# A two-layer hybrid decoder: the causal mask added on VectorE, one product for the av squares, sums and waits moved

## What is computed

```
h = rms_norm(x);  p = h @ W_in
A: u = gelu(a_u);  v = rms_norm(gelu(a_v));  y = u * (tril(w_s[g]) @ v + b_s)      # 8 groups, 4 chunks of 128 tokens
B: q, k, v from normalised latents, rotary on 32 of 96 columns, 8 heads
   softmax(q k^T * scale + causal mask) @ v                                         # 4 query blocks of 128
C: gated DeltaNet: conv(4) + silu, l2-normalised q and k, chunks of 64, 8 heads
x = x + (sum_i sigmoid(gate_i) * (y_i @ W_branch[i])) @ W_out
x = x + W2 relu(W1 rms_norm(x))^2
```

## Times and profile before

| | before |
|---|---|
| median of 3 runs | 1871.1 us (1866.58 to 1871.3) |
| the profiled execution | 1870.5 us, span 1868.7 us |
| PE busy | 1839.4 us, 98% of the span |
| DVE, ACT, POOL busy | 874.4, 467.7 and 1030.7 us |
| mean granted clock of PE | 0.994 |

### The profile page before, as it was taken

How to read it: one execution, slowest core, us unless ns; L and a number is a source line. 1 busy time by engine, 2 the same in 40 slices (tenths; PEclk the granted TensorE clock), 3 DMA queues, 4 the chain that set the end, 5 groups by cost and what they waited for, 6 DMA issues and landing times.

```text
span 1868.7 us, 26963 instructions
## 1 busy us (share of the span) xinstructions
PE 1839.4 (98%) x10428; PEld 1496.6 (80%) x10428; DVE 874.4 (47%) x1283; ACT 467.7 (25%) x872; POOL 1030.7 (55%) x580
## 2 busy tenths in 40 slices
PE   8999999999999999999999999999999999999998
PEld 7787788768888888888888777887788888888887
DVE  7787545554354322323266855465434542314141
ACT  6433314560114000000154242165501230000010
POOL 6444177225666666666654523662366666666662
PEclk9999999999999999999999999999999999999999
DMA  6212122122223232232332211321222323232332
GB/s 231 76 61 69 36 90 102 46 80 91 91 90 114 92 102 93 99 100 93 101 136 68 68 58 46 98 94 35 91 90 90 102 90 102 91 102 92 100 97 73
DMA packets 46762, 167.12 MB, mean 89 GB/s; under 512 B 5018, under 2 KB 8346, under 8 KB 46146
## 3 DMA queue, kind: packets, MB, share of 16 engines
q1 hardware_dynamic: 44066, 154.30, 24.9%
q10 hardware_dynamic: 2592, 11.29, 1.6%
HBM read 159.28 MB, written 6.29 MB: 89 GB/s over the span
## 4 chain that ended last, share of the span: by engine, by line
PE 88%; DVE 8%; ACT 2%; issue 1%; DMA 0%; SPq 0%; ACTq 0%; DVEq 0%
PE ps L445 25%; PE ps L447 25%; PE ps L446 25%; PE ps L899 2%; PE ps L922 1%; DVE lanes L1660 1%; PE ps L909 1%; DVE ps L1676 1%; DVE outer L1673 1%; PE ps L535 1%; PE ps L710 1%; PE ps L678 1%; DVE convd L1567 1%; DVE acc L1448 1%; PE ps L688 1%
## 5 line engine op out<-in xcount | busy, mean ns | idle before, releaser
L408 POOL TENSOR_SCALAR wHi<-wraw 128x1024 fp32r<-128x1024 f32 x288 | 307.7, 1068 | 786.1 <-PE ps L447 770.0
L413 POOL TENSOR_TENSOR wLo<-wraw,wHi 128x1024 fp32r<-128x1024 f32 x288 | 723.0, 2511 | 23.9
L445 PE MATMUL ps<-hHi,wHi 128*128 128x512 f32 x1360 | 546.3, 402 | 0.4 <-DVE convd L1567 0.4
L447 PE MATMUL ps<-hHi,wLo 128*128 128x512 f32 x1360 | 531.5, 391 | 0.0
L446 PE MATMUL ps<-hLo,wHi 128*128 128x512 f32 x1360 | 531.0, 390 | 0.0
L445 PEld LDWEIGHTS ps<-hHi,wHi 128*128 128x128 f32 x1360 | 256.3, 188 | 64.8 <-issue 11.1
L447 PEld LDWEIGHTS ps<-hHi,wLo 128*128 128x128 f32 x1360 | 256.0, 188 | 54.7
L446 PEld LDWEIGHTS ps<-hLo,wHi 128*128 128x128 f32 x1360 | 256.7, 189 | 49.7 <-issue 1.2
L445 PE MATMUL ps<-fHi,wHi 128*128 128x512 f32 x640 | 249.3, 390 | 0.0
L447 PE MATMUL ps<-fHi,wLo 128*128 128x512 f32 x640 | 249.1, 389 | 0.0
L446 PE MATMUL ps<-fLo,wHi 128*128 128x512 f32 x640 | 249.0, 389 | 0.0
(11 more groups left out here) (299 smaller groups left out, 2037.2 us busy)
## 6 DMA issues: line engine op xcount, KB each, us to landing
wraw<-stream SPq DMA_DIRECT2D x288, 512.0 KB, 3.4
out<-xT ACTq DMA_DIRECT2D x2, 2048.0 KB, 9.4
xT<-out ACTq DMA_DIRECT2D x2, 2048.0 KB, 7.9
xin<-x SPq DMA_DIRECT2D x4, 512.0 KB, 6.3
out<-ost ACTq DMA_DIRECT2D x1, 1024.0 KB, 4.1
out<-ost ACTq DMA_DIRECT2D x2, 512.0 KB, 3.8
prm<-params ACTq DMA_DIRECT2D x1, 647.0 KB, 3.9
prm<-params SPq DMA_DIRECT2D x1, 576.0 KB
```

The source lines that it names most:

```text
L408: nc.gpsimd.tensor_scalar(wHi[:, slot], wraw[:, slot % RAW], 1.0, 0.0, ALU.mult, ALU.add).then_inc(unit_high, 1)
L413: nc.gpsimd.tensor_tensor(wLo[:, slot], wraw[:, slot % RAW], wHi[:, slot].bitcast(F32), ALU.subtract).then_inc(unit_split, 1)
L445: mm(o, lh[lc], rh[rc], start=start, stop=False)
L447: return mm(o, ll[lc], rh[rc], start=False, stop=stop)
```

## The change

1. **Mask.** PE's product with the bf16 mask goes, and so do the two bf16 tiles and the two casts that fill them. DVE's `tensor_reduce` becomes a `tensor_tensor_reduce` that adds a row of the constants (zeros, then the mask) to the scores in place in PSUM and takes the maximum of the sum. The constants grow by 384 columns of zeros in front of the mask. The sign of the maximum now comes from a third, negated copy of the scales, one more small DVE instruction for each layer.
2. **av squares.** ACT squares the four tiles into SBUF and three PSUM banks, DVE adds them in three instructions, PE makes one product. ACT's order after attention is: output 2 rounded, Gelu table, gelu av, squares, spread sums 3, gelu au, output 3 rounded, inverse root. DVE's is: rest of output 2, inverse sums 3, `take(auT[3])`, the three sums, `normalise(3)`, rest of output 3.
3. **Spread sums** move from n % 8 = 3 to 5, behind the value products; `take_sums` to 6, `normalise` to 7, `outputs_high` to the next 0, `outputs_low` to the next 1.
4. **Spatial weights** are masked inside the merge of branch 2, between its products 6 and 7.
5. **`mix_tokens`** takes a pair: both bias products, then both groups of eight.
6. **Start.** `rotation_angles(0)` moves ahead of the layer loop; `csq` gets four buffers; sums of squares 0 to 3 come one tile later, 4 and 5 both at i = 7, 6 and 7 both at i = 8.
7. **ACT before the recurrence.** Tile z3 and the Sqrt table come before the four corner copies. `token_rows(3)` moves from k = 17 to k = 15.

```
-                    mm(bank[:, 0:w], qhT[0:QK, h, i * P:w], khT[0:QK, h, 0:w], start=True, stop=False)
-                    mm(bank[:, i * P:w], identb[:], causalb[:], start=False, stop=True).then_inc(score_done, 1)
+                    mm(bank[:, 0:w], qhT[0:QK, h, i * P:w], khT[0:QK, h, 0:w], start=True, stop=True).then_inc(score_done, 1)
...
-                    if n % 8 == 3 and n > 8:
+                    if n % 8 == 5 and n > 8:
                         spread_sums(n // 8 - 1)
...
-                    for j in range(4):
-                        pe.wait_ge(asq_ready, layer * per.asq_ready + j + 1)
-                        mm(S(0), c("ones"), asq[:, j % 2], start=j == 0, stop=j == 3).then_inc(asq_step, 1)
+                    pe.wait_ge(asq_added, layer * per.asq_added + 3)
+                    mm(S(0), c("ones"), asq[:], start=True, stop=True).then_inc(asq_step, 1)
...
                         if d2 == 0 and first == 1:
                             sum_av()
+                            pe.wait_ge(inv_copied, layer * per.inv_copied + 4)
...
-                    if 2 <= i < 9:
-                        sum_squares(i - 2)
+                    for n in {3: (0,), 4: (1,), 5: (2,), 6: (3,), 7: (4, 5), 8: (6, 7)}.get(i, ()):
+                        sum_squares(n)
...
+                take_z(3)
+                nc.scalar.preload_act_table(ACT.Sqrt)
                 for hf in range(2):
                     for ch in range(2):
...
-                take_sums(3)
+                outputs_high(2)
+                nc.scalar.preload_act_table(ACT.Gelu)
                 for j in range(4):
...
+                act.wait_ge(prob_done, layer * per.prob_done + 32)
+                act.wait_ge(pT_copied, layer * per.pT_copied + 32)
+                for j in range(4):
+                    act.wait_ge(av_ready, layer * per.av_ready + j + 1)
+                    f(S(j) if j else asq[:], avT[:, j], ACT.Square).then_inc(asq_ready, 1)
+                take_sums(3)
...
             nc.vector.tensor_scalar(tri[:], c("incl"), -1.0, None, ALU.is_ge).then_inc(tri_done, 1)
+            rotation_angles(0)
             for layer in range(DEPTH):
...
+                    if k == 15:
+                        token_rows(3)
                     if k == 17:
-                        token_rows(3)
                         take_lat(4)
...
+                    if d == 6:
+                        dve.wait_ge(tables_in, 64)
+                        tt_(p("wsp").rearrange("p (g n) -> p g n", g=8), p("wsp").rearrange("p (g n) -> p g n", g=8),
+                            c("tril").unsqueeze(1).broadcast_to([P, 8, P]), ALU.mult).then_inc(wsp_masked, 1)
...
-                    nc.vector.tensor_reduce(rowmax[:, n % 2:n % 2 + 1], S(n % 2)[:, 0:w], AX.X, ALU.max, negate=True).then_inc(row_max_done, 1)
+                    last = CST["causal"][1]
+                    nc.vector.tensor_tensor_reduce(S(n % 2)[:, 0:w], S(n % 2)[:, 0:w], cst[:, last - w:last], 1.0, NEG, ALU.add, ALU.max,
+                                                   rowmax[:, n % 2:n % 2 + 1]).then_inc(row_max_done, 1)
...
-                    if n % 8 == 5 and n > 8:
+                    if n % 8 == 7 and n > 8:
                         normalise(n // 8 - 1)
-                    if n % 8 == 7 and n > 8:
-                        outputs_low(n // 8 - 1)
+                    if n % 8 == 1 and n > 16:
+                        outputs_low(n // 8 - 2)
+                outputs_low(2)
                 invert_sums(3)
                 take(auT[:, 3], ("au", 3))
+                dve.wait_ge(score_done, layer * per.score_done + 32)
+                for j in range(3):
+                    dve.wait_ge(asq_ready, layer * per.asq_ready + j + 2)
+                    if j:
+                        dve.wait_ge(asq_added, layer * per.asq_added + j)
+                    tt_(asq[:], asq[:], S(j + 1), ALU.add).then_inc(asq_added, 1)
```

More of the change, by code:

```diff
@@ L10 @@
 I32 = mybir.dt.int32
-BF16 = mybir.dt.bfloat16
 ALU = mybir.AluOpType
@@ L97 @@
 _at = 0
-for _name, _n in (("ident", P), ("incl", P), ("ind", PAIRS * 8), ("block", P), ("ones", P), ("causal", P), ("tril", P),
+for _name, _n in (("ident", P), ("incl", P), ("ind", PAIRS * 8), ("block", P), ("ones", P), ("zeros", 3 * P), ("causal", P), ("tril", P),
                   ("freq", ROPE // 2), ("pair", PAIRS * P), ("sel", HEADS * P), ("strict", P), ("level", 6 * P), ("reset", SEQ)):
@@ L106 @@
 LOW, STACK = 32, 32 + HEADS
-FRONT, BACK = 1920, 288
+FRONT, BACK = 1664, 160
 PRM = {}
@@ L1089, in _ @@
                 nc.scalar.copy(inclr[64 * ch:64 * ch + 64], c("incl")[64 * ch:64 * ch + 64, 64 * ch:64 * ch + 64])
-            nc.scalar.copy(identr[:], ident)
-            nc.scalar.copy(identb[:], ident)
-            nc.scalar.copy(causalb[:], c("causal")).then_inc(consts_done, 1)
+            nc.scalar.copy(identr[:], ident).then_inc(consts_done, 1)
             steps = Steps()
@@ L1255, in copy_output @@
                         square_o(step // 2 - 1)
-                nc.scalar.preload_act_table(ACT.Sqrt)
                 for step in range(CHUNKS + 1):
@@ L1361, in _ @@
                     f(avT[:, j], avT[:, j], ACT.Gelu).then_inc(av_ready, 1)
-                act.wait_ge(av_ready, layer * per.av_ready + 4)
-                for j in range(2):
-                    square_av(j)
+                act.wait_ge(prob_done, layer * per.prob_done + 32)
[4 more added lines that the diff above has]
+                take_sums(3)
+                for j in range(4):
+                    if j >= 2:
+                        n = TILE_NO[("au", j)]
+                        act.wait_ge(bank_read[n % 2], layer * per.bank_read + n // 2 + 1)
+                    f(auT[:, j], auT[:, j], ACT.Gelu).then_inc(au_ready, 1)
                 outputs_high(3)
-                for j in range(2, 4):
-                    square_av(j)
-                act.wait_ge(asq_step, layer * per.asq_step + 4)
+                act.wait_ge(asq_step, layer * per.asq_step + 1)
                 inverse_root(ainv[:], S(0), 1.0 / A_WIDTH).then_inc(ainv_ready, 1)
@@ L1375, in _ @@
                 act.dma_start(xT[:].rearrange("p k s -> p (k s)"), out.rearrange("(p a) d -> p (a d)", p=P)).then_inc(x_loaded, 16)
-                for j in range(4):
-                    if j >= 2:
-                        n = TILE_NO[("au", j)]
-                        act.wait_ge(bank_read[n % 2], layer * per.bank_read + n // 2 + 1)
-                    f(auT[:, j], auT[:, j], ACT.Gelu).then_inc(au_ready, 1)
                 branch_gates(1, 1)
@@ L1609, in _ @@
                         ins.then_inc(g_token, 1)
-                    if i in (1, 5) and layer == 0:
-                        rotation_angles(i // 5)
+                    if i == 5 and layer == 0:
+                        rotation_angles(1)
                 dve.wait_ge(cum_done, layer * per.cum_done + 1)
@@ L1847, in _ @@
                 dve.wait_ge(qk_root, layer * per.qk_root + 2)
-                nc.vector.reciprocal(headstat[:, 0], headstat[:, 0]).then_inc(qkr_ready, 1)
+                nc.vector.reciprocal(headstat[:, 0], headstat[:, 0]).then_inc(vector_step, 1)
+                dve.wait_ge(vector_step, steps.next())
+                ts_(headstat[:, 2], headstat[:, 0], -1.0, None, ALU.mult).then_inc(qkr_ready, 1)
                 for m in (5, 6):
```

70 lines of the change are left out of this document (32 added, 38 removed).

## The result

The kernel with the change took 1842.8 us in the median of four runs (1840.4 to 1843.9), the kernel before 1870.4 beside it (1866.6 to 1871.3): a ratio of 0.985 with an interval of 0.984 to 0.987. The forecast was 1841, within 1834 to 1849. The profiled execution has a span of 1840.3 us in place of 1868.7, 28.4 less; the sum of the prediction was 29.2.

What follows compares the result with a forecast made beforehand. The prediction took PE, busy 98% of the span, as the bound, with DVE setting the pace in one stretch. Its terms summed to 29.2 us, taken from 1870.5 to give 1841.3; it predicted 1841, range 1834 to 1849.

Steps and rivals of the forecast that it cites:

- grouping: Bias and spread products: each change between wide fp32r and narrow float32 products costs 0.2 us; 2.0 us gained in all.
- the last spread: End of attention: PE waits 0.7 us (bounds 0 and 2) in each layer, as POOL delays DVE's rest of output 2.
- if the clock falls in places where it does not now: Anywhere on PE: one of two signs that the prediction named for being wrong; no size given.
- Start of layer 0: Third square: moving the rotary angles removes PE's 2.88 us wait and the slow clock behind it; 5.8 us, bounds 3.5 and 6.3.
- Before the recurrence: First `vnew`: the earlier table load cuts the wait from 1.46 to 0.2 us, 2.6 gained; the full clock gives 4.8 more.
- The rival that it still falls: At the recurrence: PE's clock still falls behind a short wait, the 4.8 us stay lost, 1846 in all; chance 0.18.
- token_rows(3): PE's 1.1 us wait at L821: removed, but PE waits as long at the weight load at 174.86; 0 gained.
- Mask: Attention: 64 mask products at 0.11 us go, 7.0 us gained; the last step of each layer loses 0.15, -0.3 us.
- the chain to the turn: Attention: score to turn of the probabilities spans two scores, two tile parts and a turn, 4.1 us.
- The second rival: Attention: the fused maximum takes 1.37 us at 512 columns and sets the pace; 8 us lost, 1849; chance 0.08.
- The negated scale: Before the last head copies: one small DVE instruction in idle time, costing 0.
- After attention: Av squares: one ones product for four, 4.56 us gained in each layer, less 0.7 at the last spread; 7.8 in all.

Runs made afterwards that it cites:

- the experiment that adds 0.69 us: The changed kernel with a plain row maximum of the same scores in front of each fused maximum on DVE: 1847.8 us, ratio 0.988.
- The kernel with the four edits: The changed kernel with negated scale on ACT, old order of sums, and rest of output 2 and weights' mask behind the last au take: 1838.2 us, ratio 0.983.

## Why the prediction was right

The total is right, 1.8 us below the median, and most terms stand by themselves. One step was wrong, one cost was not foreseen, and the terms for the grouping and the last spread were mis-sized. By one of its own signs the prediction was wrong: it named "if the clock falls in places where it does not now", and the clock fell in layer 1 at 978 us.

*Start of layer 0.* Right: 5.98 for 5.8. The angles do 5.2 of it; they took 4.8 us in their new place (21.0 to 25.9) and not 8.3. The prediction took the 8.3 us as work, and most of it was not. In the kernel before, the 64 columns of L1483 began 0.23 us behind a `wLo` and took 2.28 us, the three instructions of L1488 took 3.69 and L1493 0.95. In the other half of the angles, from 64.0 to 65.7 us in the same kernel, with POOL idle, the same lines take 0.19, 0.75 and 0.20. So 5.8 of the 8.3 us were DVE held by POOL, which is more than the wait of 2.88 us. By this sum, which no run tests, the wait that the change removed came from the same race as the one that it brought in.

*Before the recurrence.* Right: wait 0.17, stretch from the first L709 to the second L677 5.11 us. The clock gave back 2.2 and not 2.4 in each layer. The rival that it still falls is false, and the reason I gave (the same small waits later, at the full clock) holds up to 0.57 us.

*`token_rows(3)`.* Right: L819 comes 0.6 us sooner, and PE waits 0.56 at the next weights, 169.07. Nothing is gained.

*Mask.* Right: 6.3 us for 6.7. The fused maximum takes 0.84 us for my 0.9, and it is one pass. The half rate for two SBUF sources, which the prediction quotes, shows in no row here: `xrow<-xrow,arow` (L1599 of the kernel before, layer 1) has two of float32 and takes 0.67 us for 512 columns, and the convs at L1567, with one in PSUM, 0.75. The prediction's terms for the chain to the turn add to 3.7 us and not to its 4.1; the trace before has 3.86 (385.23 to 389.09). The second rival (1.37 us, 8 us lost) was priced too high: the experiment that adds 0.69 us, for 1.53 in all, lost 5.9 in attention.

*The negated scale: "one small instruction in DVE's idle time before the last head copies: 0".* Wrong. I had read the rule that such instructions end only after POOL's and used it for the rest of output 2, but not for this one, because it is short. Its length doesn't matter: it takes what POOL's instruction has left, up to 2.4 us, and DVE's next instruction is one that PE waits for.

*After attention.* The gain is 9.5 for 9.1. The price of the new order was a wait of 0.31 in each layer. It let the last spread start 1.35 us behind the last value products, which it follows by 0.87 in the kernel before, so the price is 0.48 and not 0.7: `wLo` was over at 387.28, and the rest of output 2, held by it (1.60 us in place of 0.73), at 387.83. The kernel with the four edits, without this wait, gains 0.49 in the same stretch.

*Grouping.* Priced at half. One group kept together saves about 0.4 us and not 0.2. From the first bias product to the next wide tile is 2.80 us in the kernel before (457.22 to 460.02) and 2.44 in the changed one (440.97 to 443.41): 0.36 for a pair, 1.5 us for the four. I had priced the 0.20 behind the second bias product (0.43 less 0.23); the other 0.16 lie at the narrow products, 1.03 and 1.02 us for two groups apart and 1.90 for the two together. The spreads show the same: attention is 4.02 us shorter, 3.13 are the mask, and 0.48 went to the last spread, so the three spreads gave 1.4 in each layer, 2.7 for my 1.2. The kernel with the mask back shows it by block, against the kernel before with the same mask: 0.35, 0.67 and 0.33 us less in the second, third and fourth.

*Clock in layer 1.* Not foreseen: the prediction put the regrouped sums at nothing beside the wait that they remove, and they put 1.6 us at risk in each layer. In the mean over the executions it is 0.4 in each.

Term by term, the two costs left out (1.6 and 1.6), the corner's 0.5 and the mask's 0.4 are balanced but for 0.8 by grouping (2.2), the products after attention (0.4), the cheaper last spread (0.4) and the start (0.2). So the sum is closer than its terms, and that is luck.

## What to carry to other kernels

Price an instruction of VectorE that has all its operands in SBUF by what GpSimd may be doing at that moment, not by its columns, and keep such ones out of the chain that TensorE waits for, on another engine or behind the urgent one. When such an instruction of few columns shows some 2 us in a trace, it was held, and its work is not what has to be hidden. When a short stall stands among small products, look at the granted clock behind it: taking the stall away may give back more than the stall. When a group of small products between two kinds is merged, count both changes of kind.

## What the runs showed of the hardware that I had not expected

The outcome of the race for VectorE's and GpSimd's ports turns within 0.05 us: 0.04 ahead, 0.18 us; 0.01 behind, 2.38 us. A copy with a scale from PSUM to SBUF (96x1024) is not held: 1.27 us beside a `wLo`. TensorE's clock fell to 1.2 GHz behind a wait of 0.96 us among 64-column products and not behind one of 0.57; and it fell with no wait at all behind 16 products of 2 columns with other small ones in some executions, and behind 24 in a row in both layers of the one that had them. A group of narrow float32 products less between wide fp32r ones saved 0.36 us at the bias products and some 0.45 at the spreads.
